# A conditioned pooling, latent-attention and expert-retrieval block: the modulation sums and the input projection in two halves of the model dimension, and the last modulation part on GpSimd in the last pass

## The chip, the cores and the metric

One core of a Trainium2 chip. The time is device microseconds of one execution of the whole program. The kernel before was run three times: 2147.86, 2151.37 and 2156.5 us, median 2151.37.

## The reference

Inputs in float32: x (256 tokens x 2048), one conditioning vector c (2048), and the weights of one layer.

```
mod = silu(c) @ ada_w + ada_b            # ada_w: 2048 x 12288
shift1, scale1, gate1, shift2, scale2, gate2 = split(mod, 6)
h = rms(x)*pre_mix_g*(1+scale1) + shift1
proj = h @ w_in                          # 2048 x 1856: 1024 pooling, 512 q, 256 kv, 64 rope
y = concat(multiscale_pool(proj[:, :1024]), latent_attention(proj[:, 1024:])) @ w_out
x = x + gate1 * rms(y)*post_mix_g
h = rms(x)*pre_ffn_g*(1+scale2) + shift2
q = h @ peer_wq                          # 2048 x 2048; scores against 128 sub-keys per half, top 16
act = gelu(h @ expert_u.T) * gate_of_the_chosen_experts     # 16384 experts
y = act @ expert_v
x = x + gate2 * rms(y)*post_ffn_g
```

Retrieval is computed densely: all 16384 experts are multiplied, and a table of gates that is zero outside the chosen ones is applied between the two products. The six parts of mod are called ada parts here: part 0 is shift1, 1 scale1, 2 gate1, 3 shift2, 4 scale2, 5 gate2.

## The kernel before, in words

The program is written engine by engine, with semaphores for every dependence; the order on each engine is the order of its code. TensorE is PE, VectorE DVE, ScalarE ACT, GpSimd POOL, SyncE SP.

**Products in three passes.** Each float32 operand is split into a rounded high part (ACT cast) and a low part (DVE subtract of the high part); PE adds high x high, high x low and low x high (`split3`, L590 to 593). So for a weight pair (two slices of 128 rows of the contraction) ACT writes `win_high`, `wout_high` or `wq_high` (L937), and DVE writes the low part back into the load's buffer (`weight_low`, L1233 to 1238).

**Loads.** `load_order` (L84 to 98) is the list of the 2 MB loads that SP issues into a ring of six buffers (L365 to 399). Load number s waits until load s-6 has been used: an ada piece until its four DVE steps are done, a weight until PE has used its last pair, `uq` until `qpe_mm` reaches 2, `ukv` until `v_mm` reaches 4 (`released`, L294 to 301). One ada part is eight pieces.

**Ada steps.** c is a column per partition, so a part is made by DVE: for each of 16 row slices and for two halves of 1024 columns, acc = ada_w slice * c + acc (`ada`, L1209 to 1231; the multiply-add is L1229). That is 32 steps for a part, 192 in all. PE then sums acc over the partitions with 16 (or, for parts 3 and 4, 32) one-column matmuls per half (`ada_columns`, L553 to 570), and DVE adds the bias and the gains (L1249 to 1265).

**Order of the stages.** (1) Parts 1 and 0, 64 steps, in the front, with the squares of x, the rope angles (L1275 to 1292) and the transposes of x beside them; (2) `modulate` and the split of h, then w_in in four column blocks, order 2, 3, 0, 1, each over all 16 slices (L609 to 635), with one ada step of part 2 behind each pair; (3) q, kv and pooling products (L642 to 675), where DVE makes the pooling groups (`pool_group`) and the rotations, PE sums part 2 (L654), and the gate1 row goes out over DRAM (L676, L1002, L1404); (4) attention, two ada steps per head; (5) w_out, 40 ada steps beside it; (6) second norm; (7) peer_wq, with one ada step of part 5 behind each pair (L1488 to 1492); (8) sub-keys, scores, and part 5 summed (L825); (9) the U pass, 128 tiles of experts, where POOL makes half of the low parts (L496); (10) the gate tables; (11) the V pass, 128 tiles, in which POOL does nothing; (12) the tail with the gate2 row, which POOL loaded from DRAM ahead of the V pass (L535).

In the V pass each tile has two half tiles in a ring of three: SP loads `raw` (L429), ACT casts (L1175), DVE subtracts (L1667), and PE multiplies (L877 to 880).

Of the kernel before, what the change touches and what calls it, by code (L numbers as in the profile page):

```python
# [11 lines left out]
P = 128  # L12
# [48 lines left out]
V_B5 = V_B2 + KT  # L61
V_PO1 = V_B5 + KT
V_PO2 = V_PO1 + KT
V_ALL = V_PO2 + KT

# [14 lines left out]
PARTS = (1, 0, 2, 3, 4, 5)  # L80
# [3 lines left out]
def load_order():  # L84

    def mixed(weights, part):
        out = []
        for p in range(PIECES):
# [3 lines left out]
    win = [("win", n, h) for n in WIN_ORDER for h in range(2)]  # L92
    wout = [("wout", n, h) for n in range(4) for h in range(2)]
    wq = [("wq", n, h) for n in range(4) for h in range(2)]
    between = ([("uq", 0, 0), ("ada", 3, 0), ("uq", 1, 0), ("ada", 3, 1), ("ukv", 0, 0), ("pool", 0, 0)]
               + [("ada", 3, p) for p in range(2, PIECES)])
    return ([("ada", 0, p) for p in range(PIECES)] + [("ada", 1, p) for p in range(PIECES)] + mixed(win, 2)
            + between + mixed(wout, 4) + mixed(wq, 5) + [("keys", 0, 0)])


def hybrid_block(nc, x, c, positions, ada_w, ada_b, pre_mix_g, post_mix_g, pre_ffn_g, post_ffn_g,
# [5 lines left out]
    for n, key in enumerate(plan):  # L107
        per_slot[n % SLOTS] += 64 if key[0] == "wq" else 16
        where[key] = (n % SLOTS, per_slot[n % SLOTS])
# [57 lines left out]
    grow = [at(f"grow{i}", o, [P]) for i, o in enumerate((M + 9216, S + 688))]  # L167
# [20 lines left out]
    ang = at("ang", M + 4096, [4, TT * HALF])  # L188
# [20 lines left out]
    gate2 = at("gate2", M + 4096, [D])  # L209
    raw = at("raw", M + 8192, [RAW, HF])  # L210
# [13 lines left out]
    with ExitStack() as ctx:  # L224
# [46 lines left out]
        y2_sq, y2_rc, y2_rs, tail_in = sem("y2_sq"), sem("y2_rc"), sem("y2_rs"), sem("tail_in")  # L271
        scaled_ready, out_stored = sem("scaled_ready"), sem("out_stored")
# [16 lines left out]
        def pair_no(kind, n, j):  # L289

            order, _, before = WEIGHTS[kind]
            return before + order.index(n) * 8 + j
# [26 lines left out]
        def high_of(kind, n, j):  # L319

            order, bufs, _ = WEIGHTS[kind]
            cols = cols_of(kind, n)
            return bufs[(order.index(n) * 8 + j) % len(bufs)][:, 0:2 * cols].rearrange("p (k n) -> p k n", k=2)
# [5 lines left out]
        U_BANK = (2, 3, 4, 5)  # L329
# [22 lines left out]

        ada_v = ada_w[0].rearrange("(p k) n -> p k n", k=KT)
# [8 lines left out]
        def _(sp):  # L362
            sp.dma_start(c_col[:], c.rearrange("o (p k) -> (o p) k", k=KT)).then_inc(c_in, 16)
            sp.dma_start(cst[:], consts[:, 0:3 * P]).then_inc(cst_in, 16)
            for s, (kind, i, h) in enumerate(plan):  # L365
                if s == 2:
                    sp.dma_start(xs[:], x[0].rearrange("(t p) d -> p t d", p=P)).then_inc(x_in, 16)
                if s == 4:
                    sp.dma_start(mask[:], consts[:, C_MASK:C_MASK + 3 * P]).then_inc(consts_in, 16)
                    sp.dma_start(freq[:], consts[:, C_FREQ:C_FREQ + HALF]).then_inc(consts_in, 16)  # L370
                    sp.dma_start(cnt[:], consts[:, C_CNT:C_CNT + 64].rearrange("p (g t) -> p g t", g=4)).then_inc(consts_in, 16)
                    sp.dma_start(i16[:], consts[:, C_I16:C_I16 + 16]).then_inc(consts_in, 16)
# [5 lines left out]
                if kind == "ada":  # L378
# [58 lines left out]
            for j in range(RING):  # L437
                sp.dma_start(raw[:, j, :], vb[j // 2, j % 2]).then_inc(v_in[j], 16)
            for j in range(RING, 6):
                load_v(j // 2, j % 2, j, j % RING)  # L440
# [7 lines left out]
        def _(pool):  # L448
# [20 lines left out]
            for m, v in enumerate((ada_b[0, 2 * D:3 * D], ada_b[0, 5 * D:6 * D], post_mix_g[0], post_ffn_g[0])):  # L469
# [61 lines left out]
            pool.wait_ge(row_stored, 32)  # L531
            pool.wait_ge(x1_stored, 16)
            pool.wait_ge(u_used, 2 * TILES)
            pool.dma_start(x1[:], x1_dram.rearrange("t p d -> p t d")).then_inc(tail_in, 16)
            pool.dma_start(gate2[:], gate_dram[1:2, :].broadcast_to([P, D])).then_inc(tail_in, 16)  # L535
            pool.wait_ge(tail_in, 32)
# [9 lines left out]
        def _(pe):  # L546
            def transpose_vectors():
                pe.wait_ge(cst_in, 16)
                pe.wait_ge(vrow_in, 208)
                pe.transpose(ps[:, 1, 0:P], vrow[:, :], ident).then_inc(vec_t, 1)  # L550
                pe.transpose(ps[:, 1, P:P + 64], vrow2[0:64, :], ident[0:64, 0:64]).then_inc(vec_t, 1)

            def ada_columns(i, bank):  # L553
# [1183 lines left out]
```

## Time and profile before

| | |
|---|---|
| median of three runs | 2151.37 us |
| the profiled execution | 2155.08 us, of which the span of the trace is 2152.3 us |
| PE busy | 1946.9 us (90%), granted clock 0.96 on the mean |
| DVE busy | 1520.1 us (71%) |
| ACT busy | 898.1 us (42%) |
| POOL busy | 432.6 us (20%) |
| moved by DMA | 437 MB, 203 GB/s over the span |

The span is what the profiler saw from the first to the last instruction. A PE that is busy is not a PE at its peak, since its matmuls overlap; the clock column of a stretch says which share of 2.4 GHz was granted (0.50 is 1.2 GHz). The stages end, in us from the start of the span: mod of the first norm 104.4, first w_in matmul 111.0, w_in 202, q/kv/pooling products 254, attention 315.4, w_out 416.6, first peer_wq matmul 437, peer_wq 550.4, U pass 565 to 1315.8, gate tables 1430, V pass 2130.5.

### The profile page before, as it was taken

How to read it: one execution, taken by the hardware profiler on the slowest of the kernel's cores; microseconds unless marked ns; L12 is line 12 of the kernel's file. 1: busy time of each engine (PE TensorE's matmuls, PEld its weight loads, DVE VectorE, ACT ScalarE, POOL GpSimd, SP SyncE). 2: the span in 40 equal slices, each digit the busy share in tenths (PEclk: the TensorE clock that was granted, in tenths of full speed). 3: DMA queues.
4: the chain of work that ended last, by engine and by line, in shares of the span. 5: the costliest groups of instructions: out<-in, count | busy, mean ns of one | idle time of the engine just before them, and what ended most of it. 6: DMA issues, size and time to landing. Idle time of an engine off the chain costs nothing.

```text
span 2152.3 us, 37807 instructions
## 1 busy us (share of the span) xinstructions
PE 1946.9 (90%) x12388; PEld 1757.5 (82%) x12388; DVE 1520.1 (71%) x2136; ACT 898.1 (42%) x1311; POOL 432.6 (20%) x290
## 2 busy tenths in 40 slices
PE   0489989798999999999999997679999999999995
PEld 0479658698999999999999997568888888888884
DVE  6897489775689999999976667975555555555554
ACT  1143233453334444444444445654444444444443
POOL 1000020000234444444444446840000000000001
PEclk9799859899999999999999999999999999999998
DMA  9989469979567676666677771045555555555553
GB/s 392 414 306 353 157 246 367 295 227 268 131 168 183 180 184 182 180 182 176 175 186 180 184 183 59 0 134 192 192 194 195 194 190 192 194 195 192 190 193 117
DMA packets 227889, 436.99 MB, mean 203 GB/s; under 512 B 23106, under 2 KB 157696, under 8 KB 214016
## 3 DMA queue, kind: packets, MB, share of 16 engines
q1 hardware_dynamic: 226240, 427.84, 63.9%
q0 software_dynamic: 1536, 8.48, 1.0%
q8 instruction: 30, 0.49, 0.1%
q14 instruction: 19, 0.16, 0.0%
q10 hardware_dynamic: 64, 0.02, 0.0%
HBM read 432.04 MB, written 4.21 MB: 203 GB/s over the span
## 4 chain that ended last, share of the span: by engine, by line
PE 79%; DVE 10%; DMA 3%; issue 3%; ACT 2%; DVEq 1%; SPq 1%; POOL 0%; ACTq 0%; POOLq 0%
PE ps L591 14%; PE ps L592 14%; PE ps L593 14%; PE ps L877 11%; PE ps L878 11%; PE ps L880 11%; DVE acc L1229 3%; DVE hotB L1636 2%; DMA ring<-in_ada_w_dram 2%; PE ps L586 2%; DMA i<-consts_dram 1%; DVEq L1636 1%; DVE ring_low L1237 1%; PE ps L568 1%; PE ps L703 1%
## 5 line engine op out<-in xcount | busy, mean ns | idle before, releaser
L591 PE MATMUL ps<-h2H,eH 128*128 128x256 f32 x2048 | 581.5, 284 | 5.8 <-DVE eL L1584 4.5
L592 PE MATMUL ps<-h2L,eH 128*128 128x256 f32 x2048 | 581.0, 284 | 0.0
L593 PE MATMUL ps<-h2H,eL 128*128 128x256 f32 x2048 | 580.9, 284 | 0.0
L1667 DVE TENSOR_TENSOR eL<-raw,eH 128x1024 fp32r<-128x1024 f32 x256 | 313.6, 1225 | 338.2 <-ACT eH L1175 338.2
L1175 ACT CAST eH<-raw 128x1024 fp32r<-128x1024 f32 x256 | 269.9, 1055 | 385.4 <-PE ps L880 379.8
L496 POOL TENSOR_TENSOR eL<-raw,eH 128x1024 fp32r<-128x1024 f32 x128 | 311.4, 2433 | 572.9 <-ACT eH L1101 572.9
L877 PE MATMUL ps<-eH,aH 128*128 128x512 f32 x1024 | 399.2, 390 | 3.6 <-DVE eL L1667 3.6
L591 PEld LDWEIGHTS ps<-h2H,eH 128*128 128x128 f32 x2048 | 394.6, 193 | 6.7 <-DVE eL L1584 5.2
L878 PE MATMUL ps<-eL,aH 128*128 128x512 f32 x1024 | 398.9, 390 | 0.0
L593 PEld LDWEIGHTS ps<-h2H,eL 128*128 128x128 f32 x2048 | 394.7, 193 | 0.0
L592 PEld LDWEIGHTS ps<-h2L,eH 128*128 128x128 f32 x2048 | 394.6, 193 | 0.0
L1593 DVE STREAM_TRANSPOSE raw<-raw 128x1024 f32<-128x1024 f32 x256 | 317.4, 1243 | 87.2 <-DMA raw<-in_peer_u_dram 79.0
L1101 ACT CAST eH<-raw 128x1024 fp32r<-128x1024 f32 x256 | 267.2, 1045 | 199.6 <-PE ps L593 160.1
L880 PE MATMUL ps<-eH,aL 128*128 128x512 f32 x1024 | 315.7, 389 | 0.0
L1229 DVE SCALAR_TENSOR_TENSOR acc<-ring,c_act,acc 128x1024 f32<-128x1024 f32 x180 | 227.1, 1295 | 23.1 <-DMA ring<-in_ada_w_dram 20.9
L877 PEld LDWEIGHTS ps<-eH,aH 128*128 128x128 f32 x1024 | 192.7, 188 | 43.8 <-issue 3.7
L880 PEld LDWEIGHTS ps<-eH,aL 128*128 128x128 f32 x1024 | 192.5, 188 | 40.1
L878 PEld LDWEIGHTS ps<-eL,aH 128*128 128x128 f32 x1024 | 192.6, 188 | 39.9
L1584 DVE TENSOR_TENSOR eL<-raw,eH 128x1024 fp32r<-128x1024 f32 x128 | 155.9, 1218 | 39.1 <-ACT eH L1101 38.5
L350 POOL TENSOR_TENSOR result<-x,scaled 128x2048 f32<-128x2048 f32 x1 | 4.5, 4474 | 712.7 <-DVEq L1687 712.7
L1116 ACT ACTIVATE acts<-ps 128x256 f32 (+1 forms) x128 | 49.2, 384 | 225.0 <-PE ps L593 225.0
L591 PE MATMUL ps<-h2H,wq_high 128*128 128x256 f32 x256 | 76.2, 297 | 13.6 <-DVE ring_low L1237 11.5
(254 smaller groups left out, 2313.1 us busy)
## 6 DMA issues: line engine op xcount, KB each, us to landing
raw<-in_peer_u_dram SPq DMA_DIRECT2D x1024, 128.0 KB, 3.0
raw<-in_peer_v_dram SPq DMA_DIRECT2D x256, 512.0 KB, 3.4
ring<-in_ada_w_dram SPq DMA_DIRECT2D x48, 2048.0 KB, 19.9
ring<-in_w_out_dram SPq DMA_DIRECT2D x8, 2048.0 KB, 11.9
ring<-in_peer_wq_dram SPq DMA_DIRECT2D x32, 512.0 KB, 15.5
ring<-in_w_in_dram SPq DMA_DIRECT2D x6, 2048.0 KB, 14.7
ring<-in_w_uq_dram SPq DMA_DIRECT2D x2, 1536.0 KB, 9.0
ring<-in_w_in_dram SPq DMA_DIRECT2D x2, 1280.0 KB, 11.7
```

What stands on the lines that cost most here:

```text
L496: pool.tensor_tensor(by_k(eL[:, j % RING, :]), turned(raw[:, j % RAW, :]), by_k(eH[:, j % RING, :].bitcast(F32)), ALU.subtract).then_inc(u ...
L591: pe.matmul(o, lh, rh, start=start, stop=False, skip_group_check=True)
L592: pe.matmul(o, lh, rl, start=False, stop=False, skip_group_check=True)
L593: return pe.matmul(o, ll, rh, start=False, stop=stop, skip_group_check=True)
L877: pe.matmul(o[n], lh, vh[n], start=start, stop=False, skip_group_check=True)
L878: pe.matmul(o[n], lh, vl[n], start=False, stop=False, skip_group_check=True)
L880: mm = pe.matmul(o[n], ll, vh[n], start=False, stop=stop, skip_group_check=True)
L1101: act.copy(by_k(eH[:, j % RING, :]), turned(raw[:, j % RAW, :])).then_inc(u_hi, 1)
L1175: act.copy(eH[:, slot, :], raw[:, slot, :]).then_inc(v_hi, 1)
L1229: ins = dve.scalar_tensor_tensor(a, w, c_act[:, k:k + 1], a, ALU.mult, ALU.add)
L1593: dve.transpose(raw[:, j % RAW, :], raw[:, j % RAW, :]).then_inc(u_tr, 1)
L1667: dve.tensor_tensor(eL[:, slot, :], raw[:, slot, :], eH[:, slot, :].bitcast(F32), ALU.subtract).then_inc(v_lo, 1)
```

## The change

`PARTS` becomes (None, None, 2, 3, 4, 5): the first two groups of 32 ada steps now hold shift1 and scale1 together, group 0 for the first 1024 model columns and group 1 for the last 1024 (each piece is two loads of 1 MB). The w_in blocks each run over the first eight slices, then, behind group 1, over the last eight. Part 5 is taken out of peer_wq: its sixteen slices are loaded as `piece` (1 MB each, three by SP ahead of the V pass, thirteen by POOL), and POOL multiplies and adds them in the V pass; DVE transposes and reduces the sum behind tile 60 and tile 62, POOL folds the quarters, stores the row, loads it back to all partitions and applies bias and gain there. The sum of part 2 moves in front of w_out and the gate1 row into its first block; the rope angles move into w_in, and the constants' loads from SP to ACT. Ada steps, in DVE's order: front 34, first half of w_in 30, then 2; second half of w_in 16; behind pooling group 1: 6; behind group 2: 4; behind group 3: 12; attention 18; w_out 38; peer_wq none.

The load order:

```
+    low, high = [], []
+    for m, n in enumerate(WIN_ORDER):
+        low += [("win", n, 0), ("ada", 1, 2 * m), ("ada", 1, 2 * m + 1)]
+        high += [("win", n, 1), ("ada", 2, m)]
+    between = ([("uq", 0, 0), ("ada", 2, 4), ("uq", 1, 0), ("ada", 2, 5), ("ukv", 0, 0), ("pool", 0, 0),
+                ("ada", 2, 6), ("ada", 2, 7)] + [("ada", 3, p) for p in range(PIECES)])
+    return ([("ada", 0, p) for p in range(PIECES)] + low + high
+            + between + mixed(wout, 4) + wq + [("keys", 0, 0)])
```

PE, from the front to w_out (`win_half(n, half)` holds the loop over eight slices):

```
             transpose_vectors()
-            ada_columns(0, 0)
...
-            ada_columns(1, 0)
+            ada_columns(0, 0, 0)
...
+            for n in WIN_ORDER:
+                win_half(n, 0)
+            ada_columns(1, 7, HI_COLS, False)
+            for n in WIN_ORDER:
+                win_half(n, 1)
                 if n == 0:
                     pe.wait_ge(lat_diag, 4)
...
-            ada_columns(2, 0)
             ring_arrived(pe, ("ukv", 0, 0))
...
-            gate_rows(0, 1)
...
+            ada_columns(2, 0, 2 * KT)
             for n in range(4):
                 for k in range(KT):
+                    if n == 0 and k == 8:
+                        gate_rows(0, 1)
...
-            ada_columns(5, 3)
```

DVE, from the first norm to peer_wq:

```
+            inputs(0)
             for n in WIN_ORDER:
+                for j in range(4):
+                    if n != 2 or j >= 2:
+                        weight_low("win", n, j)
+                    if (n, j) != (1, 3):
+                        ada(2)
+            ada(2)
+            input_columns(1, 7, HI_COLS)
+            inputs(1)
+            for n in WIN_ORDER:
+                for j in range(4, 8):
...
+                    if n != 2 or j >= 6:
+                        weight_low("win", n, j)
+                    if n == 1 and j == 5:
                         dve.wait_ge(lat_sq, 3)
...
                             dve.nop().then_inc(lat_diag, 1)
                     ada(1)
+                    if n == 1 and j == 4:
+                        angles()
...
             pool_group(1, WINDOWS[1])
+            ada(6)
...
             pool_group(2, WINDOWS[2])
+            ada(4)
             dve.wait_ge(qpe_mm, 2)
...
             pool_group(3, WINDOWS[3])
-            gate_column(0, 2, 0, V_B2, V_PO1)
-            ada(6)
+            ada(12)
...
                         weight_low("wq", n, j)
-                    ada(1)
```

POOL, behind the gate tables:

```
+            for k in range(KT):
+                pool.wait_ge(*piece_done(k))
+                w = piece[k % 3][:]
+                if k == 0:
+                    pool.tensor_scalar(sums2[:], w, c_act[:, 0:1], None, ALU.mult).then_inc(piece_step, 1)
+                else:
+                    pool.tensor_scalar(w, w, c_act[:, k:k + 1], None, ALU.mult).then_inc(half_chain, 1)
+                    pool.wait_ge(half_chain, k)
+                    pool.wait_ge(piece_step, k)
+                    pool.tensor_tensor(sums2[:], sums2[:], w, ALU.add).then_inc(piece_step, 1)
+                if k + 3 < KT:
+                    pool.wait_ge(piece_step, k + 1)
+                    load_piece(pool, k + 3)
```

DVE in the V pass:

```
+            v_tile(60, 0, False)
+            dve.wait_ge(piece_step, KT)
+            dve.transpose(sums2[:], sums2[:]).then_inc(sums_turned, 1)
+            v_tile(61, 1, False)
+            v_tile(62, 2, False)
+            dve.wait_ge(sums_turned, 1)
+            dve.tensor_reduce(quarter[:], sums2[:].rearrange("p (b l) -> p b l", l=QUAD), AX_X,
+                              ALU.add).then_inc(quarter_ready, 1)
```

## Rows read from the trace of the kernel before

**Rows 1.** Windows by stage: us, busy of each engine (instructions), PE clock, DMA share, GB/s
```profile
104.40:111.00 6.60, 0.00 (x0) 0.01 (x1) 5.41 (x13) 3.42 (x5) 0.00 (x0) 0.50 1.02 411
...
202.00:254.00 52.00, 49.55 (x202) 37.48 (x203) 23.84 (x63) 14.34 (x39) 0.00 (x0) 0.93 0.49 182
254.00:315.40 61.40, 46.91 (x140) 30.32 (x138) 44.04 (x68) 22.76 (x61) 11.65 (x8) 0.53 0.55 206
315.40:416.60 101.20, 101.14 (x640) 82.71 (x640) 88.76 (x85) 39.66 (x51) 1.48 (x2) 0.96 0.99 341
...
437.00:550.40 113.40, 99.77 (x773) 98.18 (x772) 78.43 (x69) 39.56 (x54) 0.00 (x0) 0.92 0.90 232
...
1430.00:2130.50 700.50, 698.13 (x3072) 577.62 (x3072) 356.53 (x384) 308.09 (x383) 0.00 (x0) 1.00 0.57 192
```

**Rows 2.** Timeline of DVE in the front: start, us, instructions, idle before and its releaser
```profile
10.50 1.42 DVE L1227 TENSOR_SCALAR acc<-ring,c_act 128x1024 f32<-128x1024 f32 x2 [10.50 <-DMA ring<-in_ada_w_dram]
...
25.57 4.87 DVE L1229 SCALAR_TENSOR_TENSOR acc<-ring,c_act,acc 128x1024 f32<-128x1024 f32 x4 [5.06 <-DMA ring<-in_ada_w_dram]
...
34.65 0.20 DVE L1291 TENSOR_SCALAR ang<-ang 128x64 f32<-128x64 f32 x1
```

**Rows 3.** Windows inside w_in: block 2, then block 1
```profile
122.00:138.00 16.00, 16.00 (x71) 13.03 (x70) 14.75 (x14) 5.67 (x6) 0.00 (x0) 1.00 0.58 211
...
180.00:201.00 21.00, 21.00 (x180) 21.00 (x180) 16.79 (x22) 5.25 (x5) 0.00 (x0) 1.00 0.99 396
```

**Rows 4.** Chain that ended last: start, us, what
```profile
97.42 6.97 PE ps L568 x32
...
145.54 1.20 DVE acc L1229
146.74 0.74 DVE ring_low L1237
...
224.56 4.06 PE ps L568 x32
...
506.81 1.14 DVE ring_low L1237
```

**Rows 5.** Timeline of DVE between w_in and attention
```profile
224.60 0.42 DVE L1357 TENSOR_TENSOR tmpr<-ps,trig 128x256 f32<-128x256 f32 x1 [13.90 <-PE ps L586]
...
235.27 0.18 DVE L1383 TENSOR_TENSOR zT<-catT,uT 128x16 f32<-128x16 f32 x1
```

**Rows 6.** Timeline of PE there: the pooling products
```profile
238.23 7.07 PE L586 MATMUL ps<-zT,ring 128*128 128x256 f32 x32
```

**Rows 7.** Timeline of SP's issues there
```profile
224.59 38.98 SPq L379 DMA_DIRECT2D ring<-in_ada_w_dram  x6
```

**Rows 8.** DMA issues, 220 to 262 us: count, KB each, median us to landing
```profile
ring<-in_ada_w_dram SPq DMA_DIRECT2D x3, 2048.0 KB, 8.6
```

**Rows 9.** DMA issues of the whole span: the gate rows' loads to all partitions
```profile
gate<-gate_dram POOLq DMA_DIRECT2D x2, 1024.0 KB, 8.5
```

**Rows 10.** Window of peer_wq's first 13 us, columns as in rows 1
```profile
437.00:450.00 13.00, 9.59 (x69) 9.42 (x68) 9.48 (x12) 9.88 (x16) 0.00 (x0) 0.83 0.48 158
```

**Rows 11.** Groups by line, 430 to 550.4 us: busy, mean ns, idle before and its releasers
```profile
L1229 DVE SCALAR_TENSOR_TENSOR acc<-ring,c_act,acc 128x1024 f32<-128x1024 f32 x30 | 38.4, 1280 | 14.1 <-DMA ring<-in_ada_w_dram 14.1
```

**Rows 12.** Costliest groups of the whole span, columns as in rows 11
```profile
L1667 DVE TENSOR_TENSOR eL<-raw,eH 128x1024 fp32r<-128x1024 f32 x256 | 313.6, 1225 | 338.2 <-ACT eH L1175 338.2
L1175 ACT CAST eH<-raw 128x1024 fp32r<-128x1024 f32 x256 | 269.9, 1055 | 385.4 <-PE ps L880 379.8
...
L1593 DVE STREAM_TRANSPOSE raw<-raw 128x1024 f32<-128x1024 f32 x256 | 317.4, 1243 | 87.2 <-DMA raw<-in_peer_u_dram 79.0
...
L1584 DVE TENSOR_TENSOR eL<-raw,eH 128x1024 fp32r<-128x1024 f32 x128 | 155.9, 1218 | 39.1 <-ACT eH L1101 38.5
...
L350 POOL TENSOR_TENSOR result<-x,scaled 128x2048 f32<-128x2048 f32 x1 | 4.5, 4474 | 712.7 <-DVEq L1687 712.7
```

**Rows 13.** Page, part 6: the V pass's loads: count, KB each, median us to landing
```profile
raw<-in_peer_v_dram SPq DMA_DIRECT2D x256, 512.0 KB, 3.4
```

More of the change, by code:

```diff
@@ L60 @@
 V_B2 = P
[L61 to L64, printed above, removed]
+V_PO1 = V_B2 + KT
+V_ALL = V_PO1 + KT
 TWO_PI_A = 6.28125
@@ L209, in hybrid_block @@
     gate2 = at("gate2", M + 4096, [D])
+    piece = [at(f"piece{i}", M + 2048 * i, [D]) for i in range(3)]
+    sums2 = at("sums2", M + 6144, [D])
+    quarter = at("quarter", S + 1712, [KT * 4])
+    quarters = at("quarters", M + 6144, [4, KT * 4])
+    half2 = at("half2", M + 6400, [3, KT * 4])
+    extra = at("extra", M + 6144, [D])
     raw = at("raw", M + 8192, [RAW, HF])
@@ L291, in pair_no @@
             order, _, before = WEIGHTS[kind]
+            if kind == "win":
+                return before + (j // 4) * 16 + order.index(n) * 4 + j % 4
             return before + order.index(n) * 8 + j
@@ L377, in _ @@
                 ks = slice(8 * h, 8 * h + 8)
-                if kind == "ada":
+                if kind == "ada" and i < 2:
+                    for k in range(2):
+                        sp.dma_start(dst[:, k * D:(k + 1) * D].rearrange("p (m n) -> p m n", m=2),
+                                     ada_v[:, 2 * h + k, 0:2 * D].rearrange("p (m n) -> p m n", m=2)
+                                     [:, :, i * 1024:(i + 1) * 1024]).then_inc(done, 16)
+                elif kind == "ada":
                     sp.dma_start(dst[:].rearrange("p (k n) -> p k n", k=2),
@@ L438, in _ @@
                 sp.dma_start(raw[:, j, :], vb[j // 2, j % 2]).then_inc(v_in[j], 16)
+            sp.wait_ge(u_used, 2 * TILES)
+            for k in range(3):
+                load_piece(sp, k)
             for j in range(RING, 6):
@@ new lines, in _ @@
+            pool.wait_ge(quarter_ready, 1)
+            for q in range(4):
+                pool.dma_start(quarters[0:QUAD, q, :], quarter[q * QUAD:(q + 1) * QUAD, :]).then_inc(quarters_in, 16)
+            pool.wait_ge(quarters_in, 64)
+            for i in range(2):
+                pool.tensor_tensor(half2[0:QUAD, i, :], quarters[0:QUAD, 2 * i, :], quarters[0:QUAD, 2 * i + 1, :],
+                                   ALU.add).then_inc(half_chain, 1)
+            pool.wait_ge(half_chain, KT + 1)
@@ new lines, in _ @@
+            ada(18)
+            ada(2)
+            input_columns(0, 0, 0)
+            dve.wait_ge(xn_out, KT)
+            inputs(0)
+            for n in WIN_ORDER:
+                for j in range(4):
+                    if n != 2 or j >= 2:
+                        weight_low("win", n, j)
+                    if (n, j) != (1, 3):
+                        ada(2)
+            ada(2)
+            input_columns(1, 7, HI_COLS)
+            inputs(1)
+            for n in WIN_ORDER:
+                for j in range(4, 8):
+                    if n != 2 or j >= 6:
+                        weight_low("win", n, j)
+                    if n == 0 and j == 7:
```

269 lines of the change are left out of this document (147 added, 122 removed).

## The prediction

> **What bounds the kernel now.** I read the windows by stage first, then the timeline of DVE and the chain of waits inside the stages that the change touches, and last the groups and the DMA issues for its new work. To see in the stage windows: w_out and the V pass keep PE busy throughout, peer_wq does so for 99.8 of 113.4 us, and the stretch ahead of w_in has no PE work at all and a full DMA [rows 1]. In the front DVE is the bound: 2 MB pieces arrive about 5.0 us apart (10.50 to 25.57 us holds two ada pieces and x) [rows 2], and DVE needs four steps of 1.20 us, 4.8 us, for each [rows 4]; both are nearly full, and only then can w_in start. In w_in PE is the bound at full clock: 71 wide matmuls in 16.0 us (0.225 us each) and 180 narrow ones in 21.0 us (0.117 us each) [rows 3]. In peer_wq the last part's steps wait 14.1 us for their loads [rows 11], and as a step stands behind every pair on DVE, PE waits with it.
>
> **1. The front and the first half of w_in.** 32 steps instead of 64 stand ahead of the first w_in matmul. Pieces arrive 5.0 us apart, x among the first: the eighth near 51 us, the two extra steps' piece, two loads later, near 61. The column sums of group 0 take 6.97 us (the price at the lower clock, [rows 4]) beside them, so mod is there at 64.5 us, and the first matmul 6.6 us later, as from 104.40 to 111.00 [rows 1], near 71. From 64.5 DVE has its first eight slices of h (8 us), 32 steps (38.4 us) and 14 low parts, ten of 1.14 and four of 0.74 us [rows 4], 14.4 us: 61 us, to 125. The loads push this out a little. The third w_in load waits until PE has used the first, near 85 us, when the buffers ahead are all taken; from there loads follow each other at 5.0 us, and the last steps' piece is the eighth of that row: 85 + 2 + 8 x 5.0 less 2 for w_in's two shorter ones, 127. With its two steps DVE is done at 130. Column sums at 4 to 7 us, the small additions 1 us: **mod of the second half at 137**, first matmul of that half at 142.
>
> **2. The second half of w_in.** DVE from 137: h 8 us, 16 steps 19.2, 14 low parts less the two in h 12, angles 16 instructions of 0.20 us [rows 2], 3.2, statistics and diagonals 2.4: 45 us, to 182. PE from 142: four pairs of 12 x 0.225 = 2.7, four of 1.75 (by their 320 of 512 columns), eight of 24 x 0.117 = 2.8: 40.2 us, to 182. Both would end at 182, but they are chained: behind block 0 PE waits for `lat_diag`, which DVE now makes only behind the second pair of block 1. From the last low part of block 0 (near 169) DVE issues step, low part, step, angles, low part, diagonals: 1.2 + 1.1 + 1.2 + 3.2 + 1.1 + 1.8 = 9.6 us, to 178.5; PE is through block 0 at 172. It loses 6, then has the turn of the latents (2.7 us, estimated from its 24 small matmuls) and four pairs, 11.2: **w_in ends at 192.5**, and at 194 with two cold starts of PE, behind 137 and behind this wait. Before it was 202: -8 us. Bounds: -18, where waits and cold starts cost nothing, and +3.
>
> **3. Between w_in and attention.** The column sums of part 2 leave this stretch: -4.06 us [rows 4]. But a new wait comes in. `ada(4)`, steps 24 to 27 of part 2, stands on DVE ahead of the rotations of q, and its piece ("ada", 2, 6) takes the buffer of `uq`, which is free when `qpe_mm` is 2: that is 224.60, 22.6 us behind the end of w_in [rows 5, 7], where before DVE started its rotations at once. Landing takes 8.6 us [rows 8], the four steps 4.8: the rotations and pooling group 3 behind them, all done at 235.27 before, 33.4 us behind w_in [rows 5], come 13.4 us later, at 46.8. PE starts the pooling products at 238.23 [rows 6], 36.2 behind w_in; without the column sums it would be 32.1, and group 3's come 5.2 later, at 37.3. It waits 9.5 us there. So the stretch is 52 - 4.1 + 9.5 = 57.4, with 1.5 of it again for a lowered clock and 1 less for the gate row's copy: **58 instead of 52, +6 us**. The 12 steps behind group 3 (14.4 us) end near the first scores and are hidden; if the loads behind ("ada", 2, 6) come late, up to 3 us of attention.
>
> **4. Attention and w_out.** Attention is the same 61.4 us at a clock of 0.53 [rows 1]. The sums of part 2 now stand between attention and w_out, at the clock that attention leaves: +7.0 [rows 4], of which w_out, which then starts warm, gives back 1: **+6 us**. The gate1 row's load, 8.5 us [rows 9], now starts some 12 us into w_out and is needed some 25 us into it: no cost, up to 5 if it lands behind the ring's loads (DMA share 0.99, [rows 1]).
>
> **5. peer_wq.** Gone are 32 steps and 16.8 MB of loads, so six of its eight loads stand in the ring ahead of it. Left is PE: 768 matmuls at 0.117 us [rows 3], 89.6 us. The first pairs go at the pace of the norm: 69 matmuls in 13 us, 5 us lost [rows 10], of which the two steps at its end explain half. With 2.8 us kept for that the stage is 92.4 against 113.4 [rows 1]: **-21 us**. Bounds: -24 and -14, the latter if only the waits for ada loads go. The sub-keys' load is earlier, cover for the rest. Part 5's column sums go too: **-4.0**, at the full-clock price [rows 4].
>
> **6. The V pass.** PE holds it: 700.5 us for 128 tiles, 5.47 us a tile, 2.74 a half tile [rows 1]. Of half tile g ACT may cast when g-3 is used, and cast plus subtract are 1.06 + 1.23 = 2.3 us [rows 12], so 3.2 of 5.5 us are slack. POOL's work: 15 pairs of a multiply and an add of 2048 columns and one multiply; the add costs 4.47 us, the multiply at most that [rows 12]: 139 us, with waits 160, against 60 tiles or 328 us until DVE asks. DVE's transpose (2 x 1.24) and the reduction, about 2.2 by the same rate, fit into the slack one at a time. Loads: 16.8 MB beside a DMA share of 0.57 [rows 1] for those 160 us; a V load of 3.4 us [rows 13] may come 1.3 to 2.6 us late against a slack of 2.1 us (2.74 + 2.74 + 0.4 less 3.4, less 0.4 for aH). I take **+1 us**; bounds 0 and 13 loads at 1 us, +13. GpSimd's subtract in the U pass bears on contention: DVE's own subtract takes 1218 ns beside it and 1225 without it [rows 12]. By the Trainium skill, GPSIMD Engine Reference, Key points, GpSimd shares its SBUF interfaces with VectorE and contends with VectorE instructions that have two SBUF inputs, as this subtract has; by that rule the V pass would stretch, by the two rows above it would not.
>
> **Sum.** -8 + 6 + 6 - 21 - 4 + 1 = -20. The profiled execution took 2155.1 us (span 2152.3), 3.7 above the median; a difference carries over, so from the median 2151.4: **2131 us**, 0.9% faster. Changes below 0.5%, about 11 us, are what a measurement of this kernel can't tell from none. So the gain is peer_wq's; what the halves win in the front (8) is paid back by two late waits and a cold sum.
>
> **Rivals.** (a) *The halves pay in full:* the two waits of steps 2 and 3 are covered, because DVE runs ahead or loads land sooner. For it: DVE stood idle for 13.9 us ahead of the rotations [rows 5]. Against: both stand in the order of the code. It gives -6 for `lat_diag`, -9.5 for the piece, -1.5: 2114 us. (b) *peer_wq stays bound by its loads:* its 512 KB quarters move slowly. 232 GB/s at a share of 0.90 are 258 when busy, half of it ada at up to 411 [rows 1], which leaves 188 GB/s or 11.1 us for 2 MB, where PE asks one each 11.2 us; against it, six of eight can land ahead. Then -14, and POOL's pieces or the gate row cost 5 more: 2143 us, no difference to be told. (c) *Slower: the V pass's subtract queues behind POOL.* If each subtract waited for one POOL instruction of 4.47 us, a half tile would take DVE 5.9 us instead of PE's 2.74; it decides from a subtract of 1.23 + 3.2 = 4.4 us on. For POOL's 139 us that is 24 half tiles at 3.2 us, +76: 2207 us. Against it speak the two rows of step 6.
>
> **Chances.** Forecast 0.55, (a) 0.2, (b) 0.15, (c) 0.05, 0.05 for the rest. Faster by over 0.5% (below 2140.6): forecast but for its upper tail, and (a): 0.75; within 0.5%: (b) and that tail, 0.18; slower 0.07. The range takes (a) at its end and half of (b): 2111 to 2144.
>
> **What would show it.** In the changed kernel: first w_in matmul near 71; PE waiting for the diagonals' turn behind block 0 by 6 us; DVE waiting for an ada load in front of the rotations by about 8 us and PE behind it by 9; 32 sums of 7 us ahead of w_out; peer_wq near 92 us with no wait for ada; the V pass within 2 us of 700.5, DVE's subtract at 1.23 us. Wrong if attention starts before 245, if peer_wq takes over 100, or if the V pass grows by 10.

## The result and the profile after

The changed kernel takes **2218.2 us** (2214.3 to 2218.7, 4 runs) against 2150.6 us (2147.9 to 2156.5, 4 runs) of the kernel before on the same chip: ratio 1.031, 95% interval 1.029 to 1.033. It is 3.1% slower, where 2131 us and 0.9% faster was forecast, outside the range of 2111 to 2144. The profiled execution's span is 2217.0 us against 2152.3, 64.7 more. The runs below were measured on several chips, on which the kernel before took 2150.6 to 2155.9 us in the median, so a difference in us between two of them can be off by some 5 us; the ratios are to the kernel before on the same chip.

Windows by stage of the changed kernel, columns as in [rows 1]: the front, the first half of w_in with the wait behind it, its second half; then the stretch to the first softmax operation, attention with the column sums behind it, w_out; peer_wq, the U pass, the gate tables and the V pass.

```profile
0.00:69.50 69.50, 17.93 (x99) 17.41 (x99) 44.52 (x51) 15.75 (x29) 6.44 (x16) 0.85 1.00 386
69.50:137.10 67.60, 52.72 (x320) 47.80 (x320) 55.20 (x53) 13.88 (x16) 0.00 (x0) 0.88 0.90 344
...
142.00:197.60 55.60, 48.36 (x312) 44.94 (x312) 46.15 (x68) 20.58 (x36) 0.00 (x0) 0.89 0.68 272
197.60:258.90 61.30, 46.62 (x179) 33.77 (x180) 42.67 (x77) 15.64 (x40) 0.00 (x0) 0.92 0.55 212
258.90:323.40 64.50, 49.36 (x161) 35.06 (x162) 50.52 (x73) 24.00 (x62) 11.74 (x9) 0.54 0.78 307
323.40:427.20 103.80, 103.63 (x641) 84.73 (x641) 80.94 (x80) 37.75 (x49) 0.58 (x1) 0.93 0.92 306
...
448.60:544.00 95.40, 91.76 (x772) 90.98 (x771) 41.55 (x36) 39.36 (x52) 0.00 (x0) 1.00 0.53 111
556.30:1297.80 741.50, 739.02 (x6150) 738.13 (x6150) 624.22 (x929) 315.89 (x393) 311.10 (x128) 1.00 0.66 180
1297.80:1432.90 135.10, 79.12 (x515) 66.47 (x514) 131.81 (x323) 80.44 (x198) 115.21 (x135) 0.90 0.11 41
1432.90:2193.30 760.40, 718.55 (x3072) 584.54 (x3071) 464.45 (x384) 304.46 (x380) 174.08 (x52) 0.98 0.56 197
```

The last two stages of the kernel before, cut in the same way (last product of the U pass to first of V, and the V pass from first to last product):

```profile
1312.90:1432.60 119.70, 75.71 (x515) 63.52 (x515) 116.70 (x323) 80.14 (x198) 94.41 (x130) 0.98 0.06 23
1432.60:2130.00 697.40, 697.40 (x3071) 577.28 (x3071) 354.46 (x382) 305.49 (x380) 0.00 (x0) 1.00 0.57 191
```

To see here: up to the end of the U pass the changed kernel is **15.1 us ahead** (1297.8 against 1312.9). Then the gate tables take 15.4 us more and the V pass 63.0, and 1.4 go in the tail: 64.7. In the V pass DVE has the same instructions as before but two, and 110 us more of busy time (464.45 against 354.46). PE, which was busy throughout, idles for 41.9 us, and its busy time is 21 us longer for the same products. The granted clock is 0.98 over the stage and not 1.00, which accounts for some 14 of the 21 (697.4 / 0.98 = 711.6, an estimate); the rest isn't explained.

Inside the V pass the loss lies in two places. Windows of the changed kernel:

```profile
1432.90:1500.00 67.10, 56.93 (x216) 43.61 (x215) 64.27 (x27) 20.66 (x27) 64.69 (x17) 0.91 0.61 219
1500.00:1560.00 60.00, 46.72 (x180) 35.19 (x180) 57.15 (x23) 18.70 (x24) 58.18 (x15) 0.94 0.61 218
1560.00:1620.00 60.00, 50.97 (x211) 40.13 (x212) 49.29 (x30) 20.50 (x26) 34.64 (x8) 0.97 0.51 176
1620.00:1760.00 140.00, 140.00 (x619) 115.94 (x618) 72.14 (x78) 61.67 (x77) 0.00 (x0) 1.00 0.55 194
...
1830.00:1870.00 40.00, 30.63 (x114) 24.07 (x113) 18.13 (x15) 10.72 (x14) 11.63 (x7) 0.83 0.73 242
```

While POOL is busy (64.69 of 67.10 us, 58.18 of 60), DVE is busy nearly throughout and PE has gaps. As soon as POOL is done, PE is full. The second place, 1830 to 1870, is the late chain: x1, the gate row and the bias are loaded there.

What DVE does meanwhile, from the timeline of the changed kernel (start, us, instructions), DVE first, then POOL in the same 15 us:

```profile
1433.48 4.77 DVE L1764 TENSOR_TENSOR aL<-acts,aH 128x256 fp32r<-128x256 f32 x1
1438.17 2.35 DVE L1769 TENSOR_TENSOR eL<-raw,eH 128x1024 fp32r<-128x1024 f32 x2
1440.44 3.86 DVE L1764 TENSOR_TENSOR aL<-acts,aH 128x256 fp32r<-128x256 f32 x1
```

```profile
1432.81 5.16 POOL L566 TENSOR_TENSOR sums<-sums,piece 128x2048 f32<-128x2048 f32 x1
...
1438.90 6.86 POOL L563 TENSOR_SCALAR piece<-piece,c_act 128x2048 f32<-128x2048 f32 x1
```

The small subtract for the low part of the activations, 0.42 us of work (its mean without POOL, below), takes 4.77 us and ends at 1438.25, just after POOL's add ends at 1437.97. The next ends at 1444.30 inside the multiply, after 3.86 us. Between them, while POOL issues a load and for the first 1.6 us of its multiply, DVE gets two subtracts of 1.2 us done. So here the add held the subtract until it ended, the multiply for a part of its time. The large subtracts are held too: the longest took 5.63 us where 1.22 is usual. The one-hot tables in the stage before are held as well, DVE and then POOL:

```profile
1408.33 1.24 DVE L1738 TENSOR_SCALAR hotB<-cst,slotT 128x128 f32<-128x128 f32 x4
...
1410.09 5.94 DVE L1738 TENSOR_SCALAR hotB<-cst,slotT 128x128 f32<-128x128 f32 x4
...
1416.55 10.15 DVE L1738 TENSOR_SCALAR hotB<-cst,slotT 128x128 f32<-128x128 f32 x4
```

```profile
1409.93 5.44 POOL L561 TENSOR_SCALAR sums<-piece,c_act 128x2048 f32<-128x2048 f32 x1
...
1416.33 5.44 POOL L563 TENSOR_SCALAR piece<-piece,c_act 128x2048 f32<-128x2048 f32 x1
1421.86 4.49 POOL L566 TENSOR_TENSOR sums<-sums,piece 128x2048 f32<-128x2048 f32 x1
```

Four one-hot tables that take 1.24 us before POOL begins take 5.94 beside its first multiply and 10.15 beside the next two instructions: 13.6 us of the stage's 15.4. These instructions (TENSOR_SCALAR, one tensor as input) the multiply held to its end: 1415.37, and the last of the four are done at 1416.03. Groups of the changed kernel over the whole span, columns as in [rows 12]:

```profile
L1769 DVE TENSOR_TENSOR eL<-raw,eH 128x1024 fp32r<-128x1024 f32 x256 | 365.2, 1432 | 290.6 <-ACT eH L1255 290.6
...
L1764 DVE TENSOR_TENSOR aL<-acts,aH 128x256 fp32r<-128x256 f32 x128 | 110.2, 861 | 0.5 <-ACT aH L1248 0.5
```

and POOL's new work between 1298 and 1850 us:

```profile
L563 POOL TENSOR_SCALAR piece<-piece,c_act 128x2048 f32<-128x2048 f32 x15 | 93.9, 6258 | 0.6
L566 POOL TENSOR_TENSOR sums<-sums,piece 128x2048 f32<-128x2048 f32 x15 | 72.6, 4840 | 1.2
```

### The profile page after: what moved, and what is told of

It reads as the page before. It is cut to its first block, busy times and chain, and to the rows that moved or that the text cites. A ratio compares the mean times of both kernels' runs of the same rounds, so it can differ in the third digit from the quotient of the medians.

```text
span 2217.0 us, 37768 instructions
## 1 busy us (share of the span) xinstructions
PE 1966.9 (89%) x12355; PEld 1762.6 (80%) x12355; DVE 1608.9 (73%) x2107; ACT 899.3 (41%) x1311; POOL 625.5 (28%) x344
## 4 chain that ended last, share of the span: by engine, by line
PE 73%; DVE 12%; DMA 6%; issue 5%; ACT 2%; DVEq 1%; SPq 0%; POOL 0%; ACTq 0%; POOLq 0%
PE ps L650 13%; PE ps L652 13%; PE ps L651 13%; PE ps L938 9%; PE ps L941 9%; PE ps L939 9%; DMA ring<-in_ada_w_dram 4%; DVE hotB L1738 3%; DVE acc L1306 2%; DVE eL L1769 2%; DMA raw<-in_peer_v_dram 2%; PE ps L645 1%; DVE ring_low L1314 1%; DVEq L1738 1%; PE ps L763 1%
## 5 line engine op out<-in xcount | busy, mean ns | idle before, releaser
L1769 DVE TENSOR_TENSOR eL<-raw,eH 128x1024 fp32r<-128x1024 f32 x256 | 365.2, 1432 | 290.6 <-ACT eH L1255 290.6
L938 PE MATMUL ps<-eH,aH 128*128 128x512 f32 x1024 | 408.3, 399 | 45.6 <-DVE eL L1769 45.6
L939 PE MATMUL ps<-eL,aH 128*128 128x512 f32 x1024 | 404.2, 395 | 0.0
L1306 DVE SCALAR_TENSOR_TENSOR acc<-ring,c_act,acc 128x1024 f32<-128x1024 f32 x150 | 188.6, 1297 | 34.1 <-DMA ring<-in_ada_w_dram 31.4
L1687 DVE TENSOR_TENSOR eL<-raw,eH 128x1024 fp32r<-128x1024 f32 x128 | 154.3, 1206 | 47.5 <-ACT eH L1182 47.4
L1764 DVE TENSOR_TENSOR aL<-acts,aH 128x256 fp32r<-128x256 f32 x128 | 110.2, 861 | 0.5 <-ACT aH L1248 0.5
L1738 DVE TENSOR_SCALAR hotB<-cst,slotT 128x128 f32<-128x128 f32 x256 | 95.1, 479 | 9.4 <-ACT acts L1197 9.4
```

Source lines behind the costliest of these rows:

```text
L938: pe.matmul(o[n], lh, vh[n], start=start, stop=False, skip_group_check=True)
L939: pe.matmul(o[n], lh, vl[n], start=False, stop=False, skip_group_check=True)
L1306: ins = dve.scalar_tensor_tensor(a, w, c_act[:, k:k + 1], a, ALU.mult, ALU.add)
L1769: dve.tensor_tensor(eL[:, slot, :], raw[:, slot, :], eH[:, slot, :].bitcast(F32), ALU.subtract).then_inc(v_lo, 1)
```

## The experiments

My theory after this reading (**hold**): a large POOL instruction keeps DVE from the memory that both work on, and a DVE instruction beside it gets done late or only when it ends. Rivals: the **loads** of the slices come between V's own and its raw tiles arrive late; or it is the **amount** of work in the stage, whoever does it; or the two engines share a **bandwidth**, so that each column that POOL handles costs DVE the same.

### Taking out the arithmetic, the loads, or one kind of instruction

```
 v_no_pool_math
-  pool.tensor_scalar(w, w, c_act[:, k:k + 1], None, ALU.mult).then_inc(half_chain, 1)
+  pool.nop().then_inc(half_chain, 1)
-  pool.tensor_tensor(sums2[:], sums2[:], w, ALU.add).then_inc(piece_step, 1)
+  pool.nop().then_inc(piece_step, 1)
                        (and for k = 0 the first multiply becomes a memset of the sum)
 v_no_piece_loads       (arithmetic stays; only the first three slices are loaded)
-  if k + 3 < KT:
-      pool.wait_ge(piece_step, k + 1)
-      load_piece(pool, k + 3)
 v_adds_only            the first replacement alone
 v_multiplies_only      the second replacement alone
```

> Changed kernel with POOL's multiplies and adds of the sixteen pieces left out (gate2 is therefore not computed; the sum is set to zero once); all sixteen loads and the steps behind the sum stay. Interface theory (a DVE subtract with two SBUF inputs cannot run while a POOL tensor instruction holds the shared interface): V pass 705 to 715 us, gate tables 114 to 117 instead of 131.6, whole 2140 to 2150. Load theory (V loads come late behind the piece loads): V pass 745 or more, whole 2185 to 2205.

> Changed kernel with the thirteen piece loads on POOL's queue left out: the multiplies and adds work on the three resident pieces again and again (gate2 is wrong). Interface theory: 2205 to 2220, V pass 750 or more, gate tables 131. Load theory: V pass near 705, whole 2155 to 2165.

> Changed kernel with the fifteen in-place multiplies left out, the adds kept. If only POOL instructions with two inputs hold DVE: nearly all of the V pass's 63 us stays less what the shorter stretch saves, 2190 to 2210, gate tables 114 to 122. If any POOL tensor instruction holds it, in proportion to its time (adds 15 x 4.9 us, multiplies 15 x 6.5): 43% of the loss, 2165 to 2180.

> Changed kernel with the fifteen adds left out, the multiplies kept. If only two-input POOL instructions hold DVE: 2140 to 2155, gate tables 114 to 117. If any does, by its time: 57% of the loss, 2180 to 2195, gate tables near 130.

| run | us | ratio (95%) | mean ns of DVE's `eL`, `aL` in V |
|---|---|---|---|
| changed | 2218.2 | 1.031 (1.029 to 1.033) | 1432, 861 |
| no POOL arithmetic | 2165.1 | 1.005 (1.003 to 1.006) | 1244, 417 |
| no loads of slices | 2218.2 | 1.029 (1.026 to 1.032) | 1504, 658 |
| adds only | 2201.7 | 1.021 (1.018 to 1.024) | 1360, 602 |
| multiplies only | 2177.6 | 1.010 (1.007 to 1.013) | 1315, 423 |

The arithmetic is worth 53.1 us, and the loads nothing that the noise lets through while it is there: the rival of the loads falls as the main cause. But without arithmetic 2165 us remain, between the two cases that were expected, some 25 us over a kernel without the part (2139.6, below). With nothing to pace them, thirteen loads go out between 1410 and 1450 us; by the windows of that kernel PE is idle for 12.5 us between 1412 and 1500 us, and for 8.8 us around the late chain (1760 to 1850).

The adds cost more than the multiplies (36.6 against 12.5 us over the run without either), though one takes POOL less time (4.8 against 5.7 us in these two runs). The adds alone came out as expected for "only two inputs hold" (2190 to 2210). The multiplies alone, 2177.6 us, fit neither case: too slow for it (2140 to 2155), and a little faster than by their share of POOL's time (2180 to 2195). So both kinds hold DVE, the multiply less. Alone they sum to 49 of the 53.

### Shorter POOL instructions, a later start

```
 pool_quarters
-  pool.tensor_tensor(sums2[:], sums2[:], w, ALU.add).then_inc(piece_step, 1)
+  for q in range(4):
+      part = slice(q * W, (q + 1) * W)
+      last_ = pool.tensor_tensor(sums2[:, part], sums2[:, part], w[:, part], ALU.add)
+  last_.then_inc(piece_step, 1)                  (and the multiply in the same way)
 pool_late
+  pool.wait_ge(gated, T // 4)
   for k in range(KT):
```

> The same sixteen slices on POOL, each multiply and add issued as four instructions of 512 columns instead of one of 2048. If a VectorE instruction is held until the POOL instruction beside it has ended (one holder at a time), the holds are about a quarter as long (1.2 to 1.7 us instead of 4.6 to 5.7), VectorE gets in between two quarters, and most of the 53 us that the arithmetic costs comes back: 2175 to 2190 us, mean of the eL difference under 1350 ns. If the two engines share a bandwidth, so that each column that POOL handles costs VectorE the same whatever the instruction's size, or if POOL takes the interface back at once, nothing changes: 2212 to 2222 us.

> POOL waits for the last gate table before its first multiply, so its slices run some 25 us later and wholly inside the V pass. If the stage of the gate tables is longer by POOL's arithmetic (131.6 us against 114.2), that stage is back at 114 to 117 us, the V pass still costs about 764 us, and the kernel takes 2200 to 2206 us. If instead the loads of the slices lengthen it, or the V pass loses more because all fifteen slices then meet it, the time stays within 2212 to 2222 us.

**pool_quarters** took 2176.6 us (ratio 1.012, 1.009 to 1.014): 41.6 us come back with the same columns handled. Its groups in the V pass and in POOL:

```profile
L565 POOL TENSOR_SCALAR piece<-piece,c_act 128x512 f32<-128x512 f32 x60 | 116.8, 1960 | 0.6
L571 POOL TENSOR_TENSOR sums<-sums,piece 128x512 f32<-128x512 f32 x60 | 111.1, 1880 | 1.3
```

```profile
L1775 DVE TENSOR_TENSOR eL<-raw,eH 128x1024 fp32r<-128x1024 f32 x256 | 352.2, 1381 | 302.8 <-ACT eH L1261 302.6
L1770 DVE TENSOR_TENSOR aL<-acts,aH 128x256 fp32r<-128x256 f32 x127 | 76.7, 604 | 0.0
```

Now POOL is the one that is slower: 228 us of arithmetic where the long instructions took 166. DVE's holds still add up (`eL` 1381 ns; under 1350 was expected), but its subtract of the activations is down from 861 to 604 ns, and the V pass takes 725.8 us instead of 760.4: PE idles for 8.1 us of it while POOL works, where it was 32.5. So the length of one hold counts, and not only the columns that POOL handles: the rival of the shared bandwidth, with which nothing was to change (2212 to 2222 us), falls. That the short holds lie in DVE's slack is the likely reason; it was not tested by itself. **pool_late** took 2208.5 us (ratio 1.026, 1.024 to 1.028), a little above the 2200 to 2206 expected. The gate tables are back at 122.2 us from 135.1, the V pass takes 762.6. So nearly all of the tables' loss was POOL's arithmetic beside them. The V pass, with all of that arithmetic in it now, takes only 2 us more than in the changed kernel.

### Without the last part, on both kernels

```
 before_no_part5        (its loads, 32 steps, sums and row left out; gate2 from the first row)
-  out += mixed(wq, 5)                 ->  wq
-  ada(1)                                         behind each pair of peer_wq
-  ada_columns(5, 3); gate_rows(1, 3); gate_out(1, 3); gate_column(1, 5, 3, V_B5, V_PO2)
 after_no_part5         (POOL's loop, the late row and gate left out; gate2 from the first row)
-  for k in range(KT): ...
+  pool.dma_start(gate2[:], gate_dram[0:1, :].broadcast_to([P, D])).then_inc(gate2_in, 16)
```

> The kernel before with the last ada part left out altogether (its loads, its 32 steps beside the columns of peer_wq, its column sums and gate row; the second gate is read from the row of the first). It prices what taking that part out of the peer_wq stage can bring at most. By the windows of the changed kernel that stage goes from 113.4 us to 92 to 96, and the pair of stages loses 2 to 4 us more: 2125 to 2131 us. If the stage is bound by the loads of peer_wq and not by VectorE, it takes 105 us or more and the kernel 2138 to 2145.

> The changed kernel with everything of the last ada part left out (loads, POOL's arithmetic, the late row and gate). Beside the run before it without that part, it prices the first half of the change alone, the w_in in halves and the ada parts moved with it. If the loss is all in the gate tables and the V pass, these are back at 114 and 700 us and the kernel takes 2133 to 2139 us, 5 to 12 us more than the kernel before without that part: the halves of w_in gain 4 us and give back 12 at attention and w_out. If the halves pay, it is 2120 us or less and under that run.

2129.0 us (ratio 0.989, 0.987 to 0.991) and 2139.6 us (0.994, 0.992 to 0.996), the first as expected, the second 0.6 us above its range. This splits the result into three measured terms: taking the part out is worth **-22.7 us**, w_in in halves and the parts moved with it cost **+10.6**, and the part's new place costs **+78.6**; 2151.7 - 22.7 + 10.6 + 78.6 = 2218.2 (the last figure is from another chip, on which the kernel before took 2150.6). The V pass of the second kernel is the undisturbed one, with DVE's subtracts at their own price:

```profile
1418.80:2116.00 697.20, 697.20 (x3070) 577.13 (x3070) 354.15 (x382) 305.35 (x380) 0.00 (x0) 1.00 0.55 191
```

```profile
L1733 DVE TENSOR_TENSOR eL<-raw,eH 128x1024 fp32r<-128x1024 f32 x255 | 312.4, 1225 | 337.9 <-ACT eH L1219 337.9
L1728 DVE TENSOR_TENSOR aL<-acts,aH 128x256 fp32r<-128x256 f32 x127 | 53.0, 417 | 0.0
```

### The same arithmetic on DVE; the order of the front; spaced loads

```
 part5_on_dve           (POOL only issues the loads and does the late chain)
-  POOL: multiply and add of 2048 columns for k in range(KT)
+  DVE:  for tile in range(3, 51):
+            v_tile(tile, tile % 3, False)
+            k, h = divmod(tile - 3, 3)
+            if h < 2:
+                piece_half(k, h)      scalar_tensor_tensor of 1024 columns
 part5_on_dve_three_orders    as above, and
-  ada(4)                              ahead of the rotations of q
-  ada(12)
+  ada(16)                             behind pooling group 3
-  if n == 1 and j == 5: diagonals     behind weight_low; angles() at j == 4
+  if n == 1 and j == 4: diagonals     ahead of weight_low; angles() at j == 5
-  ada_columns(2, 0, 2 * KT)           behind attention
+  ada_columns(2, 0, 2 * KT)           behind scores(1)
 before_part5_on_dve          the kernel before with only part 5 moved, as in part5_on_dve
 part5_on_dve_spaced_loads    as the three orders, with the bias and gain loads and the gate row as expected below, and
-  pool.dma_start(x1[:], x1_dram.rearrange("t p d -> p t d")).then_inc(tail_in, 16)
+  for q in range(8):
+      pool.wait_ge(v_used, 2 * (80 + 3 * q))
+      tt, part = q // 4, slice(q % 4 * W, (q % 4 + 1) * W)
+      pool.dma_start(x1[:, tt, part], x1_dram[tt, :, part]).then_inc(tail_in, 16)
```

> The changed kernel with the same sixteen slices and loads in the V pass, but the arithmetic as 32 VectorE steps of 1024 columns behind the tiles 3 to 50 (two steps in three tiles), and POOL only issuing the loads. If it is POOL's large instructions that hold VectorE, and not the amount of work, the 32 steps of 1.06 us fit into VectorE's idle share of the V pass (354 of 697 us busy) and neither the gate tables nor V lose anything to them: what is left over the 2139.6 us of the kernel without this part is the loads and the late chain (17 to 25 us by the run without POOL's arithmetic, which took 2165 us; less, since the loads are now paced): 2145 to 2163 us. If the V pass cannot take 34 us of further arithmetic in either place, it is 2175 us or more.

> As the run with part 5 on VectorE, and beside it three changes of order in front of peer_wq: part 2's last steps behind the fourth pooling window, the two diagonals of the latents before the low parts and the angles, and part 2's column sums inside attention. The first half of the change loses 10.6 us (2139.6 against 2129.0 without part 5). If these are VectorE and TensorE work put ahead of work on the path (4.6 us of waiting for the latents, 7 us of loads waited for between, 6.6 us of column sums after attention), it takes 8 to 16 us less than the run beside it. If the bound there is the ring's loads (DMA share 0.9 in w_out), less than 4.

> The front of the kernel before (parts 1 to 4 and w_in as they were), with only the last part moved into the V pass, its arithmetic on VectorE, the loads and the late chain as in the changed kernel. If the front and the V pass add up, it takes the 2129.0 us of the kernel before without that part plus what the loads and the late chain cost in the run beside it (part 5 on VectorE less 2139.6): 2135 to 2150 us, 10.6 us less than that run, and at or under the 2151 us of the kernel before. If the two are not independent, it differs from that run by less than 7 or more than 14 us.

| run | us | ratio (95%) |
|---|---|---|
| part 5 on DVE | 2155.7 | 1.002 (1.000 to 1.003) |
| kernel before, part 5 on DVE in V | 2145.4 | 0.997 (0.995 to 0.998) |
| with the three orders | 2127.4 | 0.988 (0.985 to 0.991) |
| and with spaced loads | 2117.6 | 0.984 (0.982 to 0.986) |

**part5_on_dve** settles the rival of the amount of work: the same sums in the same stage, on the engine that is supposed to be short of time, and the kernel takes 62.5 us less than the changed one. **before_part5_on_dve** is 10.3 us under it, the price of the halves again (10.6): front and V pass add up.

The **three orders** bring 28.3 us, far more than the 8 to 16 expected. Chain of waits of `part5_on_dve` (start, us, what), where the front stands still:

```profile
181.15 4.53 PE ps L628 x24
197.03 1.58 ACT cT L1053 x4
...
219.69 7.74 DMA ring<-in_ada_w_dram
...
317.87 6.62 PE ps L616 x32
324.48 0.64 PE ps L639
```

and of the kernel with the three orders at the same works:

```profile
189.43 1.57 ACT cT L1053 x4
...
212.10 0.43 DVE tmpr L1446
...
298.55 0.80 PE ps L639
```

The end of w_in is 7.6 us earlier, the rotations start at 212.10 with no load waited for, and the first product of w_out comes at 298.55, 25.9 us earlier. That is nearly the whole gain. PE's waits ahead of it in `part5_on_dve` (what waited, for what: us, times, longest), for pooling group 3 and for the diagonals:

```profile
PE ps L634 <- DVEq L1473: 11.4, 1, 11.4
...
PE ps L628 <- DVEq L1436: 7.2, 1, 7.2
```

With the three orders the first is gone and the second is 0.3 us, and the column sums of 6.62 us no longer stand behind attention: 11.4 + 6.9 + 6.6 = 24.9 of the 25.9 us. The expectation had priced the same three places at 7, 4.6 and 6.6 us. For the first it took the landing of the load alone, without the four steps behind it; for the second the turn of the latents (4.53 us above), which is work, and not the wait ahead of it. From first to last product w_out itself is hardly shorter, before and with the three orders (the second window holds the start of the column sums behind it too):

```profile
324.50:421.00 96.50, 96.50 (x516) 78.01 (x516) 78.96 (x74) 33.10 (x41) 0.57 (x1) 0.96 0.93 318
```

```profile
298.60:394.50 95.90, 95.90 (x517) 77.62 (x518) 84.76 (x78) 35.37 (x46) 1.70 (x2) 0.97 0.95 326
```

None of the three orders was run alone. With them w_in in halves does pay: 2127.4 us is 18.0 less than the 2145.4 of the kernel before with part 5 in the same place (whether orders of this kind would help that kernel too wasn't tried).

In the V pass of that kernel PE is full but for one place:

```profile
1740.00:1760.00 20.00, 14.27 (x54) 11.38 (x53) 5.57 (x6) 3.86 (x6) 1.11 (x2) 0.86 0.88 295
1760.00:1800.00 40.00, 36.59 (x152) 29.66 (x151) 24.00 (x19) 16.22 (x20) 9.73 (x3) 0.94 0.57 207
```

PE is idle 9.1 us there. POOL issues the 2 MB load of x1 at 1738.14, and the gate's loads of 1 MB follow, so its late traffic is the suspect. That was the last experiment:

> As the run with the three orders, and the late transfers of the V pass spaced out: x1 in eight loads of 256 KB, one in three tiles from tile 80 on, where it was one load of 2 MB beside the first gate loads; the loads of the bias and the gain waiting for the tiles 68 and 73; the two operations on the gate row in quarters of 512 columns. In the run with the three orders TensorE was idle for 9.1 us between 1740 and 1800 us, and the V pass from first to last product took 711.8 us against 697 without part 5. If that is V's raw tiles waiting behind the 2 MB load, 7 to 10 us come back: 2117 to 2121 us, V pass 702 to 705. If any traffic of this size costs its share wherever it lies, or the quarters on POOL cost as much, it stays at 2125 to 2129.

2117.6 us, 9.7 less, and the V pass takes 702.5 us from first to last product instead of 711.8, both as expected. The same stretch now, with only the gate's loads in it, and the stretch in which the eight loads of x1 go out (1830.84 to 1944.83):

```profile
1740.00:1800.00 60.00, 59.02 (x261) 48.60 (x260) 32.91 (x33) 25.72 (x33) 8.94 (x8) 1.00 0.74 234
...
1820.00:1960.00 140.00, 140.00 (x619) 116.05 (x618) 71.63 (x77) 62.13 (x78) 4.34 (x8) 1.00 0.61 209
```

The spacing of x1, the later gate loads and the quarters were changed together, so their shares are not known. This kernel is 1.6% faster than the kernel before and 4.5% faster than the changed one. It keeps both halves of the change: w_in in halves, and the last part in the V pass.

## Why the prediction was wrong

**Steps 1 to 5: close, in part by luck.** Mod of the first half was forecast for 64.5 us and of the second for 137, with first products at 71 and 142; measured are 69.5, 137.1 and 142.0. The end of w_in was put at 194 and came at 197.6 (-4.4 and not -8): DVE had the diagonals done only at 181.55, 3 us late, and the turn of the latents took 4.6 us and not 2.7. In step 3 the wait named came (`ada(4)` ahead of the rotations, DVE idle for 14.6 us, the load landing at 228.0; PE waited 11.4 us behind it, 9.5 forecast, and 7.0 for the diagonals, 6 forecast). With both the first softmax operation is at 258.9 instead of 258.2: +0.7, -2 was forecast. Step 4's sums took 6.62 us (7.0); attention and they are 7.3 us longer, w_out 2.6 us more at a clock of 0.93: +9.9 where +6 stood. Step 5: 95.4 us (92.4), so -18.0. The two small stages beside it give +1.0 and -2.3; in the second lay part 5's column sums, 3.63 us, for which -4.0 was forecast. And the U pass is 6.4 us shorter, which no step had: before, its first 135 us ran at clocks of 0.95 and 0.98, with 3.4 us of idle PE, and now at 1.00. In all -15.1 us at the end of U, where the steps gave -21; without the U pass's share, which is luck, it would be -8.7. By the medians of the kernels without part 5 these steps together are 10.6 - 22.7 = -12.1 us. Rival (a) falls, since both waits came; the three orders, which take them away, show that its 17 us were there to be had. Rival (b) falls too: peer_wq without part 5's steps took 95.4 us, not 99.4.

**Step 6 is the one that failed**: +1 us, with bounds of 0 and +13, against 79.8 us measured (15.4 in the gate tables, 63.0 in V, 1.4 in the tail). Three things in it were wrong.

- *The evidence.* The step took DVE's subtract of 1218 ns in the U pass, beside 1225 in V, as a sign that POOL's subtract doesn't disturb it [rows 12]. Both means were right, but in the whole U pass, with 128 of each, the two instructions overlap by more than 0.3 us only once. Timeline of the kernel before, that pair and one more place, DVE and then POOL:

```profile
567.25 2.55 DVE L1584 TENSOR_TENSOR eL<-raw,eH 128x1024 fp32r<-128x1024 f32 x1
...
806.81 2.37 DVE L1528 COPY cand<-sc 128x128 f32 x2
```

```profile
566.36 2.36 POOL L496 TENSOR_TENSOR eL<-raw,eH 128x1024 fp32r<-128x1024 f32 x1 [142.54 <-ACT eH L1101]
...
806.57 2.39 POOL L496 TENSOR_TENSOR eL<-raw,eH 128x1024 fp32r<-128x1024 f32 x1 [3.37 <-ACT eH L1101]
```

  The one subtract of DVE that meets POOL's takes 2.55 us instead of 1.22: it starts 0.89 us into POOL's 2.36, and ends 1.08 us behind it. Elsewhere the two overlap by less than 0.3 us or not at all. Two copies of 128 columns that meet POOL's subtract take 2.37 us, until POOL is done. The hold stood in this trace. A mean over a group says nothing of two instructions that hardly ever overlap.
- *The place.* POOL was expected to work in V only. It starts behind its last table, while DVE still makes one-hot tables: 15.4 us, and the sum had no term for it.
- *The size of POOL's work.* 4.47 us was taken for both instructions, for the multiply as "at most that". A multiply takes 5.44 us even at its shortest, and beside DVE's subtracts the multiplies take 6.26 in the mean and the adds 4.84: 172 us with the first multiply's 5.44, not 139.

Rival (c), the slower one, had the mechanism in rough: +76 us, 2207 us, with a chance of 0.05. Its own test, a subtract that waits for one POOL instruction, decided from 4.4 us on, and DVE's large subtracts took up to 5.63 us. That its price is so near the 79.8 measured is partly luck: it put all of it into the V pass, which lost 63.0, some 9 of them around the late chain, and it reckoned with 139 us of POOL's work and not 172. The rule of the Trainium skill, GPSIMD Engine Reference, Key points, is that GpSimd shares its SBUF interfaces with VectorE and contends with VectorE instructions that have two SBUF inputs or run in a 2-port performance mode. It spoke against the change, and the rows did not refute it: where the trace doesn't show the two instructions at the same time, such a rule is the better evidence. The trace agrees for the subtracts, which have two inputs (0.42 us alone, 4.77 beside an add). The one-hot tables and the copies, with one tensor as input, were held too; in which mode they run no trace here shows.

The loads of the slices cost nothing that shows while the arithmetic paces them, as step 6 took it, but the late chain was left out: x1's 2 MB moved from ahead of the V pass into it, and the transfers around it cost 9 to 10 us (PE idle for 9.4 us between 1830 and 1870 in the changed kernel, 9.7 us back with the transfers spaced). That is a moved step whose transfer was not counted.

What stays open: why POOL's multiply lets DVE's subtract in before it ends, while it held the one-hot tables, and its add held both, to the end; and what the loads alone cost, apart from the late chain, when the arithmetic is neither on POOL nor on DVE.

## What to carry to other kernels

Before work goes to POOL, find one place in the trace where a DVE instruction and a POOL instruction of that kind overlap in time, and read DVE's duration there; group means don't show it. If DVE has idle time, give it the work in short steps between its own; if POOL must have it, use short instructions. Space large transfers out over a stage whose queue is only a few buffers deep, and put column steps behind, not ahead of, whatever the path waits for: three moved calls brought 28.3 us here, more than the 22.7 of taking the part out.

## What the runs showed of the hardware

- A DVE subtract of 128x256, 0.42 us by itself, took 4.77 us when it began beside a POOL add of 128x2048 that took 5.16. In a POOL multiply of a tensor by a scalar it was done after 3.86 us, 1.5 us before the multiply's end; that multiply took 6.86 us instead of 5.44. Four one-hot tables of 128x128, 1.24 us by themselves, took 5.94 us beside a multiply, until it ended.
- Four POOL instructions of 512 columns instead of one of 2048 cost POOL more, beside a working DVE (1.88 us for a quarter add, 7.5 for four against 4.84, and 7.8 against 6.26 for the multiply), but the kernel 41.6 us less.
- DVE's transposes in the U pass were not held: 1243 ns in the mean [rows 12], 1249 at most, also those beside a POOL subtract. Two copies were, 2.37 us for both; and the one subtract of DVE that met POOL's took 2.55 us, not 1.22.
- With PE idle for parts of a stage its granted clock fell: 0.91 in the first 67 us of the V pass and 0.83 around the late chain, and PE's busy time in the stage was 21 us more than for the same products at 1.00, some 14 of them by the mean clock of 0.98 (an estimate).
